# Gate units of a two-layer diffusion trunk: full-precision products replaced by three one-pass products, with the low halves made by GpSimd

## The reference

```python
def _layer(x, cond, lp, ffn, latent, ctx_k, ctx_v, s0):
    mod = jax.nn.silu(cond) @ lp['w_mod'] + lp['b_mod']
    sh1, sc1, g1, sh2, sc2, g2 = jnp.split(mod[:, None, :], 6, -1)
    h = x * (1 + sc1) + sh1
    mix, kb, vb, s = _mixer(h, lp, latent, ctx_k, ctx_v, s0)
    x = _ln(DN_ALPHA * x + g1 * mix, lp['ln_g'][0], lp['ln_b'][0])
    h = x * (1 + sc2) + sh2
    x = _ln(DN_ALPHA * x + g2 * ffn(h), lp['ln_g'][1], lp['ln_b'][1])

def _mixer(h, lp, latent, ctx_k, ctx_v, s0):
    z = jnp.einsum('bld,dn->bln', h, lp['w_in'])
    qa, ka, va, ra, gda, qb, kb, vb, cvi, mg = jnp.split(z, offs, axis=-1)
    ...
    y_a = (o.reshape(b_, l_, GLA_V_W) * jax.nn.silu(ra)) @ lp['w_br_gla']   # gated linear attention
    y_b = att @ lp['w_br_na']                                               # neighbourhood attention
    y_c = _conv_module(cvi, lp)                                             # depthwise conv of 31 taps
    g = jax.nn.sigmoid(mg.reshape(b_, l_, 3, D_MODEL))
    m = g[:, :, 0] * y_a + g[:, :, 1] * y_b + g[:, :, 2] * y_c
    return m @ lp['w_out'], kb, vb, jnp.stack([s_f, s_b], 1)
```

## Time and profile before

| | |
|---|---|
| median of 3 runs | 1935.33 us (1933.25 to 1942.14) |
| the profiled execution | 1940.53 us, of which the span of the engines is 1938.7 us |
| mean granted TensorE clock | 0.982 of full speed |
| TensorE, VectorE, ScalarE, GpSimd busy | 96%, 77%, 60%, 2% of the span |
| read from device memory | 526.12 MB, 273 GB/s over the span |

### The profile page before, as it was taken

One profiled execution on the slowest core, in us unless ns is written; L12 is line 12 of the kernel. 1 busy time (PEld: TensorE's weight loads), 2 busy tenths in 40 slices (PEclk: granted clock), 3 DMA queues, 4 the chain that ended last, 5 costly groups with the idle time before them and its releaser, 6 DMA issues.

```text
span 1938.7 us, 25427 instructions
## 1 busy us (share of the span) xinstructions
PE 1854.2 (96%) x9199; PEld 1430.2 (74%) x9199; DVE 1494.7 (77%) x1842; ACT 1160.8 (60%) x1358; POOL 33.6 (2%) x58
## 2 busy tenths in 40 slices
PE   4999999999999999998999999999999999999995
PEld 1786455777868864557788888888888888888884
DVE  1447967754565479576998989989999899898997
ACT  2453225444445523252877878888788788887883
POOL 2000010000000000000000000000000000000000
PEclk9999999999999999998999999999999999999998
DMA  9666335476678352344899999999999999999992
GB/s 348 228 218 217 136 137 185 162 260 217 242 267 286 131 176 103 110 189 147 303 375 357 358 346 360 368 348 357 369 331 371 350 352 364 345 366 350 356 357 87
DMA packets 227187, 529.67 MB, mean 273 GB/s; under 512 B 4968, under 2 KB 7520, under 8 KB 227120
## 3 DMA queue, kind: packets, MB, share of 16 engines
q1 hardware_dynamic: 223136, 518.01, 74.0%
q0 software_dynamic: 3072, 8.78, 1.5%
q10 hardware_dynamic: 912, 1.97, 0.3%
HBM read 526.12 MB, written 2.62 MB: 273 GB/s over the span
## 4 chain that ended last, share of the span: by engine, by line
PE 85%; DVE 8%; DMA 3%; ACT 2%; issue 1%; ACTq 0%; SPq 0%; DVEq 0%
PE ps L898 21%; PE ps L899 21%; PE ps L900 21%; PE ps L828 6%; DVE arena L2080 3%; PE ps L849 2%; PE ps L852 2%; PE ps L851 2%; PE ps L1305 2%; PE ps L885 2%; PE ps L862 2%; PE ps L1326 1%; DMA ring<-in_w_br_na 1%; DMA ring<-in_w_mod 1%; PE ps L1158 1%
## 5 line engine op out<-in xcount | busy, mean ns | idle before, releaser
L2417 DVE TENSOR_TENSOR arena_r<-ring,arena_r 128x1024 fp32r<-128x1024 f32 x672 | 802.3, 1223 | 71.5 <-ACT arena_r L1784 38.7
L1784 ACT ACTIVATE arena_r<-ring 128x1024 fp32r<-128x1024 f32 x672 | 705.5, 1060 | 172.1 <-PE ps L900 149.7
L898 PE MATMUL ps<-arena_r 128*128 128x512 f32 (+1 forms) x1720 | 677.4, 394 | 13.4 <-DVE arena_r L1838 6.1
L899 PE MATMUL ps<-arena_r 128*128 128x512 f32 (+1 forms) x1720 | 668.5, 389 | 0.0
L900 PE MATMUL ps<-arena_r 128*128 128x512 f32 (+1 forms) x1752 | 638.0, 389 | 0.0
L898 PEld LDWEIGHTS ps<-arena_r 128*128 128x128 f32 x1720 | 324.5, 189 | 82.8 <-issue 14.3
L900 PEld LDWEIGHTS ps<-arena_r 128*128 128x128 f32 x1752 | 330.2, 188 | 69.3
L899 PEld LDWEIGHTS ps<-arena_r 128*128 128x128 f32 x1720 | 324.7, 189 | 64.0 <-issue 0.2
L1838 DVE TENSOR_TENSOR arena_r<-ring,arena_r 128x1024 fp32r<-128x1024 f32 (+1 forms) x134 | 158.7, 1193 | 167.2 <-ACT arena_r L1458 166.7
L1458 ACT ACTIVATE arena_r<-ring 128x1024 fp32r<-128x1024 f32 (+1 forms) x134 | 137.6, 1033 | 178.3 <-PE ps L900 127.6
L828 PE MATMUL ps<-ring,hT 128*128 128x512 f32 x384 | 169.2, 597 | 0.0
(11 more groups left out here) (271 smaller groups left out, 1444.6 us busy)
## 6 DMA issues: line engine op xcount, KB each, us to landing
ring<-in_moe_w_gate SPq DMA_DIRECT2D x56, 2048.0 KB, 7.8
ring<-in_moe_w_up SPq DMA_DIRECT2D x56, 2048.0 KB, 8.1
ring<-in_moe_w_down SPq DMA_DIRECT2D x56, 2048.0 KB, 9.5
ring<-in_w_in SPq DMA_DIRECT2D x28, 2048.0 KB, 10.0
ring<-in_w_mod SPq DMA_DIRECT2D x24, 2048.0 KB, 8.1
ring<-in_ffd_w_gate SPq DMA_DIRECT2D x5, 2048.0 KB, 13.9
ring<-in_ffd_w_up SPq DMA_DIRECT2D x5, 2048.0 KB, 7.7
ring<-in_ffd_w_down SPq DMA_DIRECT2D x5, 2048.0 KB, 7.5
```

What stands on the lines that cost most here:

```text
L898: mm(o_, hi, w_hi[:, n], start=start, stop=False)
L899: mm(o_, hi, w_lo[:, n], start=False, stop=False)
L1784: act_(split_part(j)[0], raw_part(j), ACT.Copy).then_inc(part_hi, 1)
L2417: V.tensor_tensor(w_lo, raw_part(j), w_hi.bitcast(F32), ALU.subtract).then_inc(part_lo, 1)
```

## The change

Each gate unit is now made of one-pass products as the other units are, but with other buffers and engines.

- ScalarE rounds each quarter of a gate unit to its high half, into one of three places in the fourth ring slot (`gate_split`). GpSimd subtracts it from the raw weights and writes the low half over them, in the unit's own slot (`gate_low`).
- The activations' high half is copied to the rest of the fourth slot and to a piece of the arena, and `hm_lo` is copied over `hT`, since their old places are written during the stage. ScalarE does the three copies.
- TensorE's `mgate` makes both groups together: for each quarter eight products with the high half, and one quarter later four with the low half, 48 per unit. The turn of a modulation unit moves into the middle of it.
- All units from `qb` on keep off the fourth slot.
- On VectorE the taps 0 to 11 stand ahead of `gla_prepare(0)` and two within its wait for the exponentials; the copy of `gdaT` stands ahead of the low parts of `kb`, and single taps stand between these parts.
- On GpSimd the subtractions of two units stand ahead of the state DMAs, those of the other four behind them, with `na_loads` ahead of the last quarter.

```diff
     def mg(l, n, turn=None):
-        p("mg", l, 0, n)
+        p("mg", l, 0, n), p("mg", l, 1, n)
         if turn is not None:
             mod_turn(l, turn)
-        p("mg", l, 1, n)
...
-    return name[0] in ("br", "out", "mg5") or (name[0] == "mod" and name[2] >= 10)
+    return name[0] in ("br", "out", "qb") or name[0] in MG or (name[0] == "mod" and name[2] >= (6, 10)[name[1]]) \
+        or (name[0] == "mod" and name[1] == 1 and name[2] in (6, 7))
...
+GATE_HIGHS, GATE_PARTS = 3, 4 * len(MG)
...
+        def gate_part(l, n, q):
+
+            qs = slice(q * PART, (q + 1) * PART)
+            i = 4 * n + q
+            hs = slice((i % GATE_HIGHS) * PART, (i % GATE_HIGHS + 1) * PART)
+            return ring_r[RING - 1][:, hs], ring_r[SLOT[UIDX[MG[n], l]]][:, qs]
...
+            def gate_low(l, n, q):
+
+                pool.wait_ge(gate_hi, GATE_PARTS * l + 4 * n + q + 1)
+                w_hi, w_lo = gate_part(l, n, q)
+                pool.tensor_tensor(w_lo, gate_raw(l, n, q), w_hi.bitcast(F32), ALU.subtract).then_inc(gate_lo, 1)
...
+                for n in range(2):
+                    for q in range(4):
+                        gate_low(l, n, q)
                 await_copied(pool, "kv", l, 0, 0)
                 await_copied(pool, "kv", l, 0, 1)
                 for n in range(2):
                     pool.dma_start(new_state[0, l, n].rearrange("(h a) k v -> (a k) h v", a=2),
                                    qarg[:, 256 * n:256 * n + 256].rearrange("p (h v) -> p h v", h=HP))\
                         .then_inc(state_stored, 16)
-                na_loads(l)
+                for n in range(2, 6):
+                    for q in range(4):
+                        if (n, q) == (5, 3):
+                            na_loads(l)
+                        gate_low(l, n, q)
...
                 def mgate(n, turn=None):
-                    w = arrived((MG[n], l))
-                    tokens_times(("mg", l, 0, n), hTk(0), w)
-                    if turn is not None:
-                        mod_turn(l, turn, mrow)
-                    tokens_times(("mg", l, 1, n), hTk(1), w)
+                    outs_ = [claim("mg", l, g, n) for g in range(G)]
+
+                    def weights_high(q):
+
+                        pe.wait_ge(gate_hi, GATE_PARTS * l + 4 * n + q + 1)
+                        w_hi = gate_part(l, n, q)[0]
+                        for c in range(2):
+                            k, cs = 2 * q + c, slice(c * 512, (c + 1) * 512)
+                            for g in range(G):
+                                mm(outs_[g], gate_high(k, g), w_hi[:, cs], start=(k == 0), stop=False)
+                                ins = mm(outs_[g], hT_r[:, k * T + g * P:k * T + (g + 1) * P], w_hi[:, cs],
+                                         start=False, stop=False)
+                        ins.then_inc(gate_used, 1)
+
+                    def weights_low(q):
+
+                        pe.wait_ge(gate_lo, GATE_PARTS * l + 4 * n + q + 1)
+                        w_lo = gate_part(l, n, q)[1]
+                        for g in range(G):
+                            for c in range(2):
+                                k = 2 * q + c
+                                ins = mm(outs_[g], gate_high(k, g), w_lo[:, c * 512:(c + 1) * 512],
+                                         start=False, stop=(k == KD - 1))
+                            if q == 3:
+                                full(ins, "mg", l, g, n)
+
+                    pe.wait_ge(h_moved, 3 * l + 3)
+                    weights_high(0)
+                    for q in range(1, 4):
+                        weights_high(q)
+                        weights_low(q - 1)
+                        if q == 2 and turn is not None:
+                            mod_turn(l, turn, mrow)
+                    weights_low(3)
...
+                def gate_split(n, q):
+
+                    i = GATE_PARTS * l + 4 * n + q
+                    if q == 0:
+                        sc.wait_ge(w_loaded[SLOT[UIDX[MG[n], l]]], 16 * NTH[UIDX[MG[n], l]])
+                    if i >= GATE_HIGHS and 4 * n + q < GATE_HIGHS:
+                        sc.wait_ge(gate_used, GATE_PARTS * l)
+                        sc.wait_ge(gate_lo, GATE_PARTS * l)
+                    elif i >= GATE_HIGHS:
+                        sc.wait_ge(gate_used, i - GATE_HIGHS + 1)
+                        sc.wait_ge(gate_lo, i - GATE_HIGHS + 1)
+                    act_(gate_part(l, n, q)[0], gate_raw(l, n, q), ACT.Copy).then_inc(gate_hi, 1)
...
+                gate_split(0, 3)
                 gla_exps(0)
-                mgate(0, turn=7)
+                mod_columns(l, 7)
+                for q in range(3):
+                    gate_split(1, q)
+                gates_taken(0)
...
+                gate_split(2, 3)
+                if l == 0:
+                    mod_columns(l, 9)
+                for q in range(3):
+                    gate_split(3, q)
+                gates_taken(2)
                 gla_sqrt()
-                mgate(3)
+                gate_split(3, 3)
+                for q in range(3):
+                    gate_split(4, q)
+                gates_taken(3)
                 gla_turned(0)
                 gla_exps(1)
-                mgate(4)
+                gate_split(4, 3)
...
-                lo_unit("kb")
+                conv_taps(0, 2)
                 await_product(dv, "gda", l)
                 free(V.tensor_copy(gdaT[0:32, :], bank(("gda", l))[0:32, 0:T]), "gda", l)
+                for q in range(4):
+                    lo_part(l, "kb", q)
+                    if q < 3:
+                        conv_taps(2 + q, 3 + q)
...
+                    conv_taps(5 + g, 6 + g)
                     st.next(glog_soft)
...
                     if g:
-                        conv_taps(22, 28)
+                        conv_taps(27, 29)
+                    else:
+                        conv_taps(12, 14)
                     st.next(exps_ready)
...
+                conv_taps(7, 12)
+                dv.wait_ge(h_moved, 3 * l + 1)
                 await_product(dv, "qb", l, 1)
                 gla_prepare(0)
-                conv_taps(0, 12)
+                conv_taps(14, 16)
                 gla_mask(0)
+                conv_taps(16, 21)
                 gla_carry(0)
-                conv_taps(12, 22)
+                conv_taps(21, 27)
                 gla_norm(0)
                 gla_prepare(1)
-                conv_taps(28, TAPS)
+                conv_taps(29, TAPS)
                 gla_mask(1)
                 gla_carry(1)
                 gla_norm(1)
```

More of the change, by code:

```diff
@@ L549, in build @@
             sem(n) for n in ("diag_ready", "gate_arg", "gate_exp", "mask_ready", "sel_ready", "flag_ready", "y_ready"))
+        h_moved, gate_hi, gate_lo, gate_used = (sem(n) for n in ("h_moved", "gate_hi", "gate_lo", "gate_used"))
         dve_step, act_step, pool_step = sem("dve_step"), sem("act_step"), sem("pool_step")
@@ L1547, in _ @@
                 hi_unit("qb")
+                await_product(sc, "gda", l)
+                act_(hT_r[:, :], hm_lo.bitcast(F32), ACT.Copy).then_inc(h_moved, 1)
                 for i in range(2):
@@ L1551, in _ @@
                 mod_columns(l, 6)
+                def gate_split(n, q):
[9 more added lines that the diff above has]
+                    act_(gate_part(l, n, q)[0], gate_raw(l, n, q), ACT.Copy).then_inc(gate_hi, 1)
+                held = [n for i, n in enumerate(UNITS) if SLOT[i] == RING - 1 and i < UIDX[MG[0], l]][-1]
+                await_product(sc, *LAST[held])
+                if held in DFIRST:
+                    sc.wait_ge(part_lo, max(j for j in range(len(DQ)) if DQ[j][0] == held) + 1)
+                act_(ring_r[RING - 1][:, GATE_HIGHS * PART:4 * PART], h_hi[:, 0:PART].bitcast(F32),
+                     ACT.Copy).then_inc(h_moved, 1)
+                await_product(sc, "cum", l, 1)
+                act_(arena_r[:, 10240:10240 + PART], h_hi[:, PART:2 * PART].bitcast(F32), ACT.Copy).then_inc(h_moved, 1)
+                for q in range(3):
+                    gate_split(0, q)
                 for i in range(2):
@@ L1582, in gla_turned, with gates_taken @@
                     free(ins, "oT", l, g)
-                def mgate(n, turn=None):
+                def gates_taken(n):
                     for g in range(G):
-                        if g and turn is not None:
-                            mod_columns(l, turn)
                         take(gates[:, g * 3 * D + n * 512:g * 3 * D + (n + 1) * 512], ("mg", l, g, n), ACT.Sigmoid)
@@ L1598, in _ @@
                 gla_keys(0)
-                mgate(1, turn=None if l else 8)
+                gate_split(1, 3)
+                if l == 0:
+                    mod_columns(l, 8)
+                for q in range(3):
+                    gate_split(2, q)
+                gates_taken(1)
                 if l == 0:
                     mod_rows(l, 9, mrow)
-                mgate(2, turn=None if l else 9)
+                gate_split(2, 3)
```

(35 more changed lines are left out.)

9 lines of the change are left out of this document (added).

## The result

The changed kernel takes 1998.4 us (median of four runs, 1997.2 to 1999.5) against 1936.8; the ratio is 1.031, 95% interval 1.029 to 1.033. The forecast was 1901 and the range ended at 1960: the time lies 38 us above it. The second rival (GpSimd and VectorE hold each other up) had the right side and the right place, with too small a price.

What follows compares the result with a forecast made beforehand. It took TensorE and VectorE together to bound the gate stages. Stage gains of 15.5 and 18.5 us plus 4.2 from glog steps, less 3.6 for hand-overs, gave 34.6 off 1935.3: 1901 us, range 1892 to 1960.

Steps and rivals of the forecast that it cites:

- The second rival: Gate stages: subtractions and VectorE's two-SBUF-operand operations block each other; 1950 us, 1978 at a length of 2.7; chance 0.34.
- Beside VectorE: VectorE during GpSimd's subtractions: no loss taken per subtraction, conv operations staying at 0.398 us; other end its whole length.
- Gate products: TensorE's gate units: 48 one-pass products at 0.227 us, 10.9 us per unit, 3.05 less than 13.95.
- ScalarE: 24 copies per layer at 1.06 us plus three more, 29.7 us; free unless late VectorE holds back high quarters.
- GpSimd: 24 subtractions of 128x1024 per layer, 1.8 us each within 0.9 to 2.7; four take 7.2 against TensorE's 10.9.
- Conv taps and gdaT copy: Fourteen taps leave VectorE's path, 22 us per layer; earlier copy returns 3.5 us in layer 1, 0.7 in layer 0.
- A new wait: mg2's first low quarter waits behind the state DMAs in GpSimd's queue: 1.4 us per layer, 2.3 at length 2.7.
- The sum without a hold-up: Both gate stages: 15.5 us less in layer 0, 18.5 in layer 1; with glog and hand-overs, 34.6 gained, 1901 us.
- The first rival: Gate stages: subtractions over 2.73 us make TensorE wait for low quarters; 1917 us at 3.2, 1931 at 3.5; chance 0.21.

Runs made afterwards that it cites:

- e1: Changed kernel, but GpSimd fills each low quarter with zeros by a memset that reads nothing, in place of the subtraction: 1912.4 us, ratio 0.986.
- e2: Kernel before with only the 14 moved conv taps and the moved gdaT copy, gate units left as full-precision products: 1929.4 us, ratio 0.995.
- e10: Changed kernel with all conv taps back at their old places, everything else of the change kept: 2023.0 us, ratio 1.043.
- e5: Changed kernel with three memsets in a row, which read nothing, in place of each subtraction: 1921.8 us, ratio 0.994.
- the probe: Kernel before with 15 pairings of VectorE and GpSimd operations behind its last step; VectorE's two-SBUF-operand form took 7.31 us beside memset, 15.88 beside subtractions.

## Why the prediction was wrong

The step that failed is *Beside VectorE*: "I take nothing, by these nearest rows". In place of nothing, the runs showed a loss of 2.1 us of VectorE's time for each subtraction: VectorE's busy time per layer is 50.3 us longer with subtractions (127.8) than with memsets (77.5, e1), and each stage 42 us longer. The rows showed GpSimd issuing DMAs, and the text said itself that such an instruction does not read SBUF; they bore on the question no more than the memset of e1 does. The mutual hold-up stood on record as a rival with a chance of 0.34, but its price was taken at too short a length, and the range left out a block by longer subtractions; so it ended 38 us too low.

- *Gate products* (10.9 us): right but for the hand-overs. Without reading (e1) mg3 takes 11.3, from the end of gla_out(0) to the turn behind it:

```profile
210.21 0.37 PE ps L1076 x4
...
221.85 0.44 PE ps L897 x4
```

- *ScalarE* (1.06 us): right; 48 copies of 1.05 us, and where VectorE was on time (e1) TensorE waited 0.7 us per layer for them. The warning in that step, that a late VectorE would hold back the high quarters, came true: 10.2 us of TensorE's waits in layer 0 of the changed kernel.
- *GpSimd* (1.8, within 0.9 to 2.7): 2.31 alone (9.23/4), 2.66 in the kernel. The estimate of 2.25 from the Trainium skill (GPSIMD Engine Reference, Elementwise — side-by-side cycle accounting) was nearer than the value taken.
- *Conv taps and gdaT copy*: right. Together, without the gates, they bring 9 us (e2), and the wait for gdaT in layer 1 is gone there. The taps alone, undone in the changed kernel, cost 25 (e10).
- *A new wait* (1.4 us per layer, 2.3 at a length of 2.7): 2.4 in layer 0 of the changed kernel, 0.9 in e1, right in place and size and not what decides.
- *The sum without a hold-up* (1901): e1 measures 1912, a gain of 26.3 us over the kernel before in its own rounds where 34.6 were forecast. The forecast stages, 112.7 - 15.5 = 97.2 and 113.3 - 18.5 = 94.8, came out at 100.9 and 101.3, 10 us more, for which the sum had allowed 3.6. TensorE's waits in them are 4.0 and 5.9 us, and layer 1's clock is 0.97; how the rest divides was not measured.
- *The second rival* (1950, 1978 at 2.7 us): right in mechanism, mis-sized in the length and the number of the subtractions. It counted 20 subtractions per layer at 1.8 us and a share of 0.8, 29 us, less 4 of waits. Measured, VectorE's busy time grows by 127.8 - 77.5 = 50.3 us per layer, 2.1 for each of 24; 42.3 of them lengthen the stage in layer 0 and 41.7 in layer 1, 84 together, against 86 between the medians. In layer 0, 23 of the 24 had run by 271.5 us, ahead of gla_out(1) at 284.9, and not 20. The last counts as well, as it stretches gla_norm(1), on whose last product the end of the stage waits; here of the changed kernel and then of e1:

```profile
292.66 3.46 DVE L2200 TENSOR_TENSOR arena<-arena 128x512 f32<-128x512 f32 x1
```

```profile
250.94 0.69 DVE L2200 TENSOR_TENSOR arena<-arena 128x512 f32<-128x512 f32 x1
```

  The share of 0.8 holds at the measured length: 2.1/2.66. Put together, the 84 us of price less the 26 us of gain that e1 shows make 58; the change is 61.6 us slower.
- *The first rival* (late GpSimd) was refuted as the cause by e5; TensorE's wait for GpSimd is 2.4 us in layer 0 of the changed kernel, and 11.5 only in e10, where VectorE held GpSimd up for longer.

## What to carry to other kernels

Before work is given to GpSimd, list what VectorE does beside it. Where both engines had operations with two SBUF operands, these ran one after the other, so the work was not taken off VectorE, only made at GpSimd's pace (2.3 us for what VectorE does in 1.2). VectorE operations with a PSUM operand were free of it in the probe (7.26 us in all four pairings). And when one engine's work gets cheaper, count how much room the next engine has (here 30 to 34 us per stage) and convert only as many units as fit into it; three of six in a mended order were worth 1.2%, six of six on VectorE nothing.

## What was not expected of the hardware

A one-operand VectorE operation in SBUF was slowed by a memset that reads nothing (4.11 to 7.43 us for twelve), while the slower two-operand form was not. GpSimd's one-operand multiplication took longer than its two-operand subtraction (10.99 against 9.23 us for four). In the probe one VectorE operation came through between two subtractions; in the kernel one was held through four of them (10.48 us), though its record starts 0.8 us before the first. Why is open: two state DMAs were issued on GpSimd in that moment, and no run parted them from the subtractions. GpSimd was held longer still, through some twenty conv operations in e10 (11.40 us), while in the changed kernel a subtraction that came amid a run of 20 of them went through at once (2.51 us, at 198.18). Which engine goes first is not settled by these runs.
